# Page keys turned on VectorE in 32x32 blocks, with block-diagonal queries; turned new-token probabilities copied by ScalarE

## The reference, cut to what matters

```python
ckv_past = cache_ckv[j, page_table].reshape(Bs, past_len, KV_LORA)    # 8 x 4096 x 256
kr_past = cache_krope[j, page_table].reshape(Bs, past_len, ROPE_D)    # 8 x 4096 x 64
s_past = (einsum('nthc,nsc->nhts', q_lat, ckv_past) + einsum('nthr,nsr->nhts', q_rope, kr_past)) * MLA_SCALE
p = softmax(concatenate([s_past, s_new], -1))
ctx = einsum('nhts,nsc->nthc', p[..., :P], ckv_past) + einsum('nhts,nsc->nthc', p[..., P:], ckv_new)
```

## Time and profile before

| | |
|---|---|
| median of 3 runs | 2794.82 us (2793.02, 2794.82, 2804.56) |
| profiled execution | span 2804.0 us, 61,530 instructions |
| TensorE, weight loads | busy 2691.9 us (96%), 2491.0 us (89%) |
| VectorE, ScalarE, GpSimd | busy 1723.8 us (61%), 1111.5 us (40%), 1239.7 us (44%) |
| attention phases | 1502.92 to 1595.4, 1649.67 to 1741.1, 1795.18 to 1886.66, 1940.77 to 2032.6 us of the span |

### The profile page before, as it was taken

How to read it: one execution, slowest core, us unless ns; L and a number is a source line. 1 busy time by engine, 2 the same in 40 slices (tenths; PEclk the granted TensorE clock), 3 DMA queues, 4 the chain that set the end, 5 groups by cost and what they waited for, 6 DMA issues and landing times.

```text
span 2804.0 us, 61530 instructions
## 1 busy us (share of the span) xinstructions
PE 2691.9 (96%) x21801; PEld 2491.0 (89%) x21801; DVE 1723.8 (61%) x3199; ACT 1111.5 (40%) x2499; POOL 1239.7 (44%) x1296
## 2 busy tenths in 40 slices
PE   6999999998999999999899999999998999999998
PEld 5898999998999999999887787878788999999998
DVE  4677678665333336896546666666675434358984
ACT  5121212354444445442543333333364444444444
POOL 3000000455555566544753333333376666665544
PEclk8999999999999999999999999999999999999999
DMA  7422111635666754743133434343453343547442
GB/s 258 144 77 91 48 46 38 208 125 155 204 202 205 213 180 151 260 167 95 54 111 110 148 105 143 105 145 118 147 176 96 118 145 117 150 155 253 165 144 105
DMA packets 385187, 397.91 MB, mean 142 GB/s; under 512 B 27587, under 2 KB 346678, under 8 KB 383046
## 3 DMA queue, kind: packets, MB, share of 16 engines
q1 hardware_dynamic: 362994, 363.57, 41.0%
q10 hardware_dynamic: 13780, 23.05, 2.3%
q0 software_dynamic: 8192, 8.40, 1.0%
HBM read 291.46 MB, written 103.48 MB: 141 GB/s over the span
## 4 chain that ended last, share of the span: by engine, by line
PE 72%; DVE 14%; issue 4%; ACT 3%; POOL 2%; SPq 2%; DMA 2%; DVEq 0%; ACTq 0%; POOLq 0%
PE bank L4068 18%; PE bank L4069 18%; PE bank L4070 17%; PE bank L4691 3%; PE bank L4811 2%; PE bank L4705 2%; DVE xT L3552 1%; DVE stage L3523 1%; DVE td L3529 1%; DVE xT L3545 1%; PE bank L4197 1%; PE bank L4732 1%; POOL op_l L1407 1%; PE bank L4359 1%; PE bank L4797 1%
## 5 line engine op out<-in xcount | busy, mean ns | idle before, releaser
L1407 POOL TENSOR_TENSOR op_l<-raw,op_h 128x512 fp32r<-128x512 f32 (+1 forms) x396 | 518.7, 1314 | 419.8 <-ACT op_h L2076 405.4
L4068 PE MATMUL bank<-t_high,op_h 128*128 128x258 f32 x1736 | 497.7, 287 | 15.2 <-ACT tq L2104 7.5
L4069 PE MATMUL bank<-t_low,op_h 128*128 128x258 f32 x1736 | 493.3, 284 | 0.0
L4070 PE MATMUL bank<-t_high,op_l 128*128 128x258 f32 x1736 | 490.7, 283 | 0.0
L4068 PE MATMUL bank<-hh,whi 128*128 128x344 f32 (+3 forms) x1324 | 436.5, 330 | 20.1 <-POOL hl L1302 4.3
L4070 PE MATMUL bank<-hh,wlo 128*128 128x344 f32 (+3 forms) x1324 | 419.9, 317 | 0.0
L4069 PE MATMUL bank<-hl,whi 128*128 128x344 f32 (+3 forms) x1324 | 419.4, 317 | 0.0
L4068 PEld LDWEIGHTS bank<-t_high,op_h 128*128 128x128 f32 x1736 | 329.2, 190 | 29.1 <-issue 23.4
L4069 PEld LDWEIGHTS bank<-t_low,op_h 128*128 128x128 f32 x1736 | 331.0, 191 | 0.0
L4070 PEld LDWEIGHTS bank<-t_high,op_l 128*128 128x128 f32 x1736 | 330.5, 190 | 0.0
L4068 PE MATMUL bank<-td,op_h 128*128 128x258 f32 x1008 | 289.2, 287 | 18.4 <-DVE xT L3552 15.1
(11 more groups left out here) (521 smaller groups left out, 6241.4 us busy)
## 6 DMA issues: line engine op xcount, KB each, us to landing
raw<-in_w_gu SPq DMA_DIRECT2D x84, 512.0 KB, 4.6
pk<-in_cache_ckv SPq DMA_DIRECT2D x256, 128.0 KB, 2.4
ada_x<-in_w_ada SPq DMA_DIRECT2D x28, 1024.0 KB, 8.4
act_high<-st_all SPq DMA_DIRECT2D x86, 258.0 KB, 5.3
act_low<-st_all SPq DMA_DIRECT2D x86, 258.0 KB, 5.2
act_raw<-tq SPq DMA_DIRECT2D x164, 129.0 KB, 4.0
raw<-in_w_down SPq DMA_DIRECT2D x48, 384.0 KB, 4.3
wst<-in_w_in_even SPq DMA_DIRECT2D x28, 512.0 KB
```

The lines of the kernel that those rows point to most:

```text
L1407: nc.gpsimd.tensor_tensor(op_l[p][:, 0:t.half, :], op_source(p, t), op_h[p][:, 0:t.half, :].bitcast(F), ALU.subtract).then_inc(op_lo.sem, 1)
L4068: mm(out, wh_, xh_, start=start, stop=False, skip_group_check=more)
L4069: mm(out, wh_, xl_, start=False, stop=False, skip_group_check=more)
L4070: return mm(out, wl_, xh_, start=False, stop=stop, skip_group_check=more)
```

## The change

Page keys are no longer transposed on TensorE. VectorE's `transpose` turns each 32x32 block of a page by itself, SBUF to SBUF: tokens 32i to 32i+31 stay in partition group i, and within the group the partition is now one of 32 channels. One instruction does half a step's keys (128x1024) or rope keys (128x256), straight from `pk` or `pr` to `keyt` or `keyrt`, without bank 5. To multiply with such keys, the query weights are block-diagonal: for each of 8 key blocks and 2 rope blocks of 32 channels (`KB`, `RB`, `QB` = 10), 128 partitions by 4 x 8 columns, where partition group i has the queries in columns 8i to 8i+7 and zero elsewhere. page_scores is now 10 x 4 matmuls with 32 weight columns and 64 moving columns. Scores of token 32i + b of a page lie at partition 32g + 8i + head, column b.

The queries are first repeated over the four partition groups by 24 DMAs per pair on SyncE (`queries_repeated`): for the first pair before `tokens_saved`, for the others in step 4 of the pair before, behind the loads of step 6. VectorE multiplies them with a 0/1 mask once per sample (`query_blocks`).

The exponent's input of 64 columns is repeated over four blocks, so that its output has 256 columns as before, of which three quarters are zeroed by the same mask in `page_probs_out`, now a multiplication of 256 columns. The sum of the exponents then counts each four times, which constants of 4 and 1/4 undo. The prompt's `turned` copies move from VectorE to ScalarE. The diff, cut:

```diff
-FILLS = []
-for _d in range(STEPS):
-    FILLS += [("ropes", _d), ("keys", _d, 0)] + ([("probs", _d - 1)] if _d > 0 else []) + [("keys", _d, f) for f in (1, 2, 3)]
-FILLS += [("probs", STEPS - 1), ("peaks",), ("weights",), ("sums",)]
+FILLS = [("probs", _d) for _d in range(STEPS)] + [("peaks",), ("weights",), ("sums",)]
+GB = P // CG
+KB = CT * P // GB
+RB = ROPE // GB
+QB = KB + RB
+NEWS = 2 * GB
@@ SyncE
+            def queries_repeated(r):
+                if r > 0:
+                    sp.wait_ge(q_ready, 3 * r)
+                for i in range(CG):
+                    rows = slice(i * GB, (i + 1) * GB)
+                    for jj in range(P // GB):
+                        sp.dma_start(qrep[rows, CT * jj:CT * jj + CT], qall[jj * GB:(jj + 1) * GB, 0:CT, 2 * r:2 * r + 2, :]
+                                     ).then_inc(qrep_in.sem, 16)
+                    for jj in range(RB):
+                        sp.dma_start(qrep[rows, KB + jj], qall[jj * GB:(jj + 1) * GB, CT, 2 * r:2 * r + 2, :]).then_inc(qrep_in.sem, 16)
...
                 sp.wait_ge(knew_ready, 1)
+                queries_repeated(0)
                 tokens_saved()
...
+                        if r < PAIRS - 1 and d == 4:
+                            queries_repeated(r + 1)
@@ GpSimd, rope_step and plain_split
-                        pool.wait_ge(fill_ready, (s - 2) // STEPS * NF + FILL["ropes", (s - 2) % STEPS] + 1)
+                        pool.wait_ge(*key_ready(ropes_turned(s - 2)))
...
+                else:
+                    pool.wait_ge(ds_ready, PAIRS * (CG * STEPS) + 1)
@@ ScalarE, attention
+                def turned(u):
+                    e, q, small = unit(u)
+                    act.wait_ge(pt_bank[0], u0 + u + 1)
+                    act.wait_ge(ao_ready, u0 + u + 1)
+                    w = min(q + 1, 4)
+                    nc.scalar.copy(pt[u % 2][:, 0:w, :], bank[2][:, 0:w * P].rearrange("p (b q) -> p b q", b=w)
+                                   ).then_inc(pt_out[0], 1)
...
                     u = 2 * d
-                    ropes_out(d)
                     probs(u + 1)
                     if d > 0:
                         page_probs(d - 1)
+                    turned(u)
                     late_turned(u)
                     if u > 0:
                         output(u - 1)
-                    keys_out(d, 1)
                     if u + 2 < 2 * TB:
                         probs(u + 2)
+                    turned(u + 1)
                     output(u)
-                    keys_out(d, 3)
@@ VectorE
+            def query_blocks(r, n):
+                if n == 0:
+                    dve.wait_ge(*qrep_in(16 * CG * (P // GB + RB) * (r + 1)))
+                on = blk[:].unsqueeze(1).unsqueeze(3)
+                for dst, first, end in ((qbd_r[:], KB, QB), (qbd_k, 0, KB)):
+                    ins = v.tensor_tensor(dst, qrep[:, first:end, n, :].unsqueeze(2).to_broadcast([P, end - first, CG, MH]),
+                                          on.to_broadcast([P, end - first, CG, MH]), ALU.mult)
+                ins.then_inc(q_ready, 1)
...
+            def ropes_out(r, d):
+                dve.wait_ge(ds_ready, r * (CG * STEPS) + CG * d + 1)
+                for half in range(2):
+                    dve.wait_ge(rope_in[2 * (d % 2) + half], 64 * (r * (STEPS // 2) + d // 2 + 1))
+                    v.transpose(keyrt[:, half], pr[2 * (d % 2) + half][:].rearrange("p g c -> p (g c)")).then_inc(key_ready.sem, 1)
+            def keys_out(r, d, half):
+                dve.wait_ge(page_in[2 * (d % 2) + half], 16 + 64 * (r * (STEPS // 2) + d // 2 + 1))
+                v.transpose(keyt[half], pk[2 * (d % 2) + half][:].rearrange("p g c -> p (g c)")).then_inc(key_ready.sem, 1)
...
                     if d > 0:
                         page_maxima(r, d - 1)
-                    turned(u)
-                    keys_out(r, d, 0)
+                    if d % 4 == 0:
+                        query_blocks(r, d // 4)
+                    ropes_out(r, d)
                     if d > 0:
                         page_probs_out(r, d - 1)
...
+                    keys_out(r, d, 0)
                     if d > 0:
                         page_sums(r, d - 1)
-                    turned(u + 1)
-                    keys_out(r, d, 2)
+                    keys_out(r, d, 1)
                     low_output(u)
@@ TensorE
-                for part_ in range(CT + 1):
+                for j in range(QB):
                     for g in range(CG):
-                        q = q2[:, part_ if part_ < CT else CT + g % 2, n, :]
-                        k = keyb[:, :, (2 * g + part_) * P:(2 * g + part_ + 1) * P] if part_ < CT else keyr2[:, :, g // 2, :]
-                        ins = mm(bank[6][g * GC:g * GC + MH, 0:2 * P], q, k, start=part_ == 0, stop=part_ == CT)
+                        if j < KB:
+                            at = g * CT * P + key_block(j) * GB
+                            k = keyb[:, :, at:at + GB]
+                        else:
+                            at = g * ROPE + (j - KB) * GB
+                            k = keyrt[:, :, at:at + GB]
+                        ins = mm(bank[6][g * GC:(g + 1) * GC, 0:NEWS].rearrange("p (a b) -> p a b", a=2),
+                                 (qbd_k[:, j] if j < KB else qbd_r[:, j - KB]).rearrange("p i h -> p (i h)"), k, start=j == 0, stop=j == QB - 1)
...
-                    ropes(r, d)
                     turned(u)
-                    keys(r, d, 0)
...
-                    keys(r, d, 1)
                     turned(u + 1)
-                    weighed(u, lambda: keys(r, d, 2))
-                    keys(r, d, 3)
+                    weighed(u)
```

More of the change, by code:

```diff
@@ L490, in trunk @@
         last_sq[5] = [rs, sw[0], sw[1]]
+        os_at = used["keep"]
         os32 = lay("keep", "os32", [P, MH, NS])
@@ L513, in trunk @@
         xsd = lay("keep", "xsd", [P, KT, NS])
+        qbd_r = nc.alloc_sbuf_tensor_at("qbd_r", [P, RB, CG, MH], F, offset=at0 + os_at)
+        blk = nc.alloc_sbuf_tensor_at("blk", [P, CG], F, offset=at0 + used["late"])
+        selh = nc.alloc_sbuf_tensor_at("selh", [P, MH], F, offset=at0 + used["late"] + 32)
         used["lat"] = used["pair"] = used["tail"] = used["keep"]
@@ L572, in trunk @@
         keyb = nc.alloc_sbuf_tensor_at("keyb", [P, 2, KT * N], F, offset=w_at - KT * N * 4 - N * 4)[:, :, 0:TB * P]
-        keyt = [keyb[:, b].rearrange("p (j m) -> p j m", m=P) for b in range(2)]
-        keyr2 = keyr.rearrange("p (b a) m -> p b a m", b=2)
+        keyt = [keyb[:, b] for b in range(2)]
+        keyrt = keyr.rearrange("p k m -> p (k m)").rearrange("p (b x) -> p b x", b=2)
         free_h, free_l = (nc.alloc_sbuf_tensor_at(f"free{b}", [P, (KT - O0) * N], F, offset=w_at - b * KT * N * 4 - (KT - O0) * N * 4)
@@ L2506, in attention @@
                 u0 = r * (2 * TB)
[L2508 to L2518, removed]
                 def page_probs(d):
-                    w = 2 * P + (NS if d % 4 == 0 else 0)
                     act.wait_ge(dn_ready, r * STEPS + d + 1)
@@ L3758, in page_maxima @@
                     w += NS
-                    new = bank[6][:, 2 * P:w]
+                    new = bank[6][:, NEWS:w]
                     order(v.tensor_tensor(new, new, one(newmask[:, bass.ds(2 * r + d // 4, 1), :]), ALU.add))
@@ L3787, in page_sums @@
                 if d % 4 == 0:
-                    order.put(v.tensor_copy(total[:, n:n + 1], part_sum[:, d:d + 1]))
+                    order.put(v.scalar_tensor_tensor(total[:, n:n + 1], drop[:, d:d + 1], float(CG), part_sum[:, d:d + 1],
+                                                     ALU.mult, ALU.add))
                     ins = v.tensor_copy(accs[:, n, :], new)
@@ L3821, in normalised @@
                     v.tensor_scalar(p, p, amx[u % 2][:, 3:4], None, ALU.mult).then_inc(pn_ready, 1)
-                def turned(u):
-                    e, q, small = unit(u)
-                    dve.wait_ge(pt_bank[0], u0 + u + 1)
-                    dve.wait_ge(ao_ready, u0 + u + 1)
-                    w = min(q + 1, 4)
-                    v.tensor_copy(pt[u % 2][:, 0:w, :], bank[2][:, 0:w * P].rearrange("p (b q) -> p b q", b=w)
-                                  ).then_inc(pt_out[0], 1)
                 def low_output(u):
@@ L3967, in pairs @@
             def pairs():
+                block_masks()
                 query_low(0, 0, 2)
@@ L4671, in filled @@
                 pe.wait_ge(fill_out, r * NF + FILL[key] + 2)
-            def ropes(r, d):
-                for half in range(2):
-                    pe.wait_ge(rope_in[2 * (d % 2) + half], 64 * (r * (STEPS // 2) + d // 2 + 1))
-                fill(r, "ropes", d)
-                for i in range(4):
-                    two = pr[2 * (d % 2) + i // 2][:, 2 * (i % 2):2 * (i % 2) + 2, :].rearrange("p j c -> p (j c)")
-                    ins = nc.tensor.transpose(bank[5][:, i * P:(i + 1) * P], two, ident[:])
-                ins.then_inc(fill_ready, 1)
@@ L4683, in keys @@
-            def keys(r, d, f):
```

(16 more changed lines are left out.)

63 lines of the change are left out of this document (38 added, 25 removed).

## The result

The changed kernel takes 2813.43 us (median of 12 runs) against 2799.62 (12 runs) of the kernel before: ratio 1.0036, 95% interval 1.0021 to 1.0051. By the ratio it is slower by 10 us (13.8 by the medians), where 18.3 us less were forecast. The profiled execution has a span of 2813.1 us, 9.1 more than before.

A forecast was written before the change was run, and what follows sets the result against it. TensorE was taken to bound the attention phases, VectorE part B after the change. 35.5 us gained less 17.2 lost by three queues (8.7 + 7.5 + 1.0) gave -18.3: 2794.8 to 2776 us, range 2748 to 2824.

The forecast's parts named there:

- the first of the new queues: SyncE: 24 query DMAs per pair at 0.40 us, 9.6 us in all; first phase's page_scores later, costing 8.7 us.
- the query DMAs cost more: Rival on SyncE: 0.8 us per query DMA, 2813 us; chance 0.08 together with its opposite, costing nothing, 2760.
- part A: Page step from page_scores to page_probs on TensorE: transposes gone, 0.87 us less in six steps, 5.5 us a phase.
- part B: Page step from page_probs to next page_scores: VectorE's chain becomes the bound, 5.97 us against 6.15; 3.0 us a phase.
- The last step: Part A of a phase's last step: gain only 0.3 us, with less other TensorE work ahead of ScalarE's exponent.
- page_scores and the transpositions: page_scores on TensorE stays at 1.3 us; VectorE's transposes take 1.22 us for 128x1024 and 0.42 for 128x256.
- Slow issue of small matmuls: Rival in page_scores: 80 pairs at 28 ns, every part A 0.9 us longer, 2805 us; chance 0.22.
- slow transpositions: Rival in part B: VectorE key halves at 2.3 us each, 2.1 us more a step, 2844 us; chance 0.14.
- fast ones: Rival: VectorE transposes at the normalisation's 0.88 us, 0.7 us a step less, 2754 us; chance 0.10.
- GpSimd's pace: Rope page loads issued 1.15 us apart, 9.2 a step: 1.0 us lost in the fourth phase, nothing in the others.
- The swap to ScalarE: ScalarE takes VectorE's copies of turned new-token probabilities for three 512-wide copies: no cost; without that cover 1.1 us a step.

The follow-up runs named there:

- the run from DRAM: Changed kernel with the same 24 query DMAs a pair, read from a DRAM copy of the queries written once: 2801.41 us, ratio 0.9990.
- the copies put back on VectorE: Changed kernel with TensorE repeating the queries instead of DMAs, and both copies of turned new-token probabilities back on VectorE: 2773.87 us, ratio 0.9871.
- two attempts: No query DMAs, first key half early; fourth phase's weight splits behind rope loads: 2746.83 us; then also x reloaded ahead of loads awaiting splits: 2745.31 us.
- the four-DMA version: Changed kernel with 4 query DMAs a pair instead of 24, read from a DRAM copy in repeated order: 2764.52 us, ratio 0.9853.

## Why the prediction was wrong

**The step that failed is the first of the new queues: the price and the room of the query DMAs.** I gave 8.7 us for the first phase and 7.5 for the other three, 16.2 in all. The experiments give 60, of which the traces place 14.6 us at the start of the first phase and 41.5 around step 7 of the first three. That term alone turns the forecast of -18 into a loss. The mechanism was named, a queue that holds up what stands behind it; its size was wrong, in three places:

- *The issue.* I took 0.40 us, the gap between two included, from DMAs that write SBUF to DRAM; SBUF to SBUF costs 0.61, with the gap 0.65. In the first phase VectorE's wait is 15.6 instead of 10.3 us. The 24 for the next pair stand 17.0 to 17.6 us in the queue instead of 9.6.
- *The time at which the pages are due.* I had two steps of 10.2 us plus 1.1, 21.5 us from the end of page_values(4). In the first phase it was 17.7: that end comes late in its step, because of the new sample's work, so that 3.1 us of the step were left (1572.3 to 1575.39), then a step of 9.5 and 5.1. With 29.0 us on SyncE's side (22.7 forecast), the pages were 11.3 us late and not 1.2. With my own 22.7 us on SyncE's side they would still have been 5.0 us late, and in the run from DRAM, with 12.8 us for the 24, they were 7 to 8: the right price alone would not have saved the forecast.
- *What follows a long wait.* TensorE's clock was at its lower level after each of the three page waits, 2.0 us each time, and after the wait of the first phase, 0.7 us. The forecast had no term for that.

The rival with this mechanism ("the query DMAs cost more", 2813) had the measured time and 0.08 of the chance, together with its opposite. That its time agrees is luck: its 0.8 us each was not measured, and 2813 came of a lower price with less room, less a gain that was larger than forecast.

**The gain was under-estimated.** I gave 35.5 us, 34.5 with GpSimd's 1.0 taken off; without the query DMAs it is 50. Most of the difference is part A: 8.7 us gained in the third phase for 5.5 forecast, and 3.7 for 3.0 in part B. In step 3 part A lost 1.24 us (5.07 to 3.83), not 0.87: page_scores to its successor is 0.17 us shorter than before, and the seven transposes behind it took 0.74 us where they took 0.93. The last step falls short, as forecast, but with a gain of 0.94 us it is well above the 0.3 that I gave it (4.34 us before, 1874.65 to 1878.99, and 3.40 now, 1877.49 to 1880.89): there TensorE waits 0.49 us for ScalarE's exponent. Part B was forecast at 5.97 us and is 5.86 to 6.00 there. Its working stands, and VectorE became the bound, as the key wait ahead of page_scores and the copies put back on VectorE show. How near the next bound stood was not in the forecast: with the first key half out of the way TensorE's key wait falls from 28.0 us to 1.9, and the time by only 3 to 6.

**page_scores and the transpositions** were right: 1.25 us for 1.3, 1.24 us for 1.22, 0.43 for 0.42. Slow issue of small matmuls, slow transpositions and fast ones are all refuted by these rows.

**GpSimd's pace** was in the forecast with 1.0 us in the fourth phase; VectorE waited 4.8 there, and 7.5 without the query DMAs. A likely reason, which no run separates, is that steps of 9.7 us leave less room than steps of 10.2. The starts of the earlier trace rows are also 1.17 us apart (31 gaps in 36.21 us) and not 1.15. **The swap to ScalarE** at nothing for ScalarE holds. That the swap has no worth without the rest was not in the forecast; its 0.5 us a step arise only once VectorE bounds part B.

Not settled: which wait of the last output projection takes up the 8.5 us that VectorE no longer waits in the fourth phase, since two attempts each met the next one.

## What to carry to other kernels

A DMA whose transfer is hidden is not hidden in issue: the time for which it stands in the queue of the engine that issues it counts against everything behind it, and moving it back in that queue, as here, may only change who waits. Before adding many small DMAs, take the issue time from a row with the same kind of source and destination, and work out the due time of the next load from the actual gaps of the steps it spans, not from a mean step. Work that a fuller engine can do in half a microsecond, here TensorE repeating the queries, may be the cheaper way when a queue is the scarce thing. Work moved off an engine was worth nothing here until that engine bounded the step. And taking a wait away pays only as far as the next bound allows: 26 us less of it gave 3 to 6.

## What was not expected of the hardware

- A DMA from SBUF to SBUF with 64 pieces of 64 bytes takes SyncE 0.612 us to issue, with 32 pieces 0.593; the same shapes from DRAM take 0.427 and 0.424. From DRAM with 320 pieces it is 0.612 again (16 DMAs of the four-DMA version).
- After about 13 us without work TensorE ran on at a granted clock of 0.50 (window 1601.30 to 1609.26), and 80 small records took 2.29 us instead of 1.25. After 14.5 us in the first phase it had 0.50 as well, until 1523.6.
- 80 records of 32 weight columns and 64 moving columns, four column groups taking turns, run at 15.6 ns each, 31 ns for each matmul of two records.
